# Depthwise convolution taps of a diffusion backbone: four per pass on TensorE, fewer on GpSimd and VectorE

## The reference, cut to what matters

```python
def conformer_conv(h, w_in, b_in, w_dw, b_dw, ln_g, ln_b, w_out, b_out):
    a, g = jnp.split(h @ w_in + b_in, 2, axis=-1)
    u = a * jax.nn.sigmoid(g)
    u = lax.conv_general_dilated(u, w_dw[:, None, :], window_strides=(1,),
        padding=[(CONV_K // 2, CONV_K // 2)],
        dimension_numbers=("NWC", "WIO", "NWC"),
        feature_group_count=D_CONV) + b_dw
    # a layer norm over the channels, silu, and a product with w_out follow
```

## Time and profile before

| | |
|---|---|
| median of three runs | 1851.17 us (1850.03 to 1855.13) |
| profiled execution: span from the first to the last instruction | 1854.0 us |
| TensorE matmul busy | 1803.4 us, 97% of the span |
| VectorE busy | 1198.1 us, 65% |
| ScalarE busy | 619.6 us, 33% |
| GpSimd busy | 171.7 us, 9% |
| chain that ended last: TensorE, VectorE, GpSimd | 84%, 6%, 4% of the span |

### The profile page before, as it was taken

The page is one execution under the profiler, slowest core; times in us unless marked ns, Lnnn a source line. Parts: engine busy times, 40 slices in busy tenths (PEclk is TensorE's granted clock), DMA queues, the critical chain, the costliest instruction groups (busy, mean ns, idle before and its releaser), DMA issues.

```text
span 1854.0 us, 22066 instructions
## 1 busy us (share of the span) xinstructions
PE 1803.4 (97%) x8604; PEld 1486.5 (80%) x8604; DVE 1198.1 (65%) x1541; ACT 619.6 (33%) x796; POOL 171.7 (9%) x148
## 2 busy tenths in 40 slices
PE   5899999998999999999999999999999999999999
PEld 2688888888898888888988888889764898888888
DVE  5876767667867676666676766547798555444454
ACT  2522222234342223222432222225776542222221
POOL 0000000002110000000200000002995200000000
PEclk8999999998999999999999999999999999999999
DMA  7753634431436354363154353411120321313201
GB/s 279 273 201 114 212 127 155 185 113 47 136 114 227 114 176 164 122 218 114 69 196 145 140 200 113 136 68 46 46 91 25 116 88 69 136 68 113 90 23 69
DMA packets 160395, 238.10 MB, mean 128 GB/s; under 512 B 3805, under 2 KB 110509, under 8 KB 160204
## 3 DMA queue, kind: packets, MB, share of 16 engines
q1 hardware_dynamic: 160016, 236.99, 36.5%
q10 hardware_dynamic: 316, 0.23, 0.0%
HBM read 235.11 MB, written 2.10 MB: 128 GB/s over the span
## 4 chain that ended last, share of the span: by engine, by line
PE 84%; DVE 6%; POOL 4%; ACT 3%; DMA 1%; issue 1%; SPq 0%; POOLq 0%; DVEq 0%; ACTq 0%
PE bank L1670 15%; PE bank L1672 15%; PE bank L1677 15%; PE bank L1545 10%; PE bank L1547 10%; PE bank L1546 10%; POOL tmp_c L628 3%; DVE mod_acc L1025 2%; PE bank L1927 1%; DVE w_lo L992 1%; PE bank L1617 1%; PE bank L1615 1%; PE bank L1619 1%; DMA raw_pair<-in_w_mod 1%; POOL sq_sum L593 1%
## 5 line engine op out<-in xcount | busy, mean ns | idle before, releaser
L1670 PE MATMUL bank<-a_hi,w_hi 128*128 128x512 f32 x1408 | 551.9, 392 | 6.2 <-ACT a_hi L686 4.7
L1672 PE MATMUL bank<-a_hi,w_lo 128*128 128x512 f32 x1408 | 548.9, 390 | 0.0
L1677 PE MATMUL bank<-a_lo,w_hi 128*128 128x512 f32 x1408 | 434.5, 390 | 1.3 <-DVE a_lo L1100 1.2
L1670 PEld LDWEIGHTS bank<-a_hi,w_hi 128*128 128x128 f32 x1408 | 265.0, 188 | 63.4 <-issue 6.3
L1218 DVE SCALAR_TENSOR_TENSOR h<-bank,half_gate,h 128x512 f32<-128x512 f32 x320 | 233.3, 745 | 121.7 <-PE bank L1547 121.1
L1677 PEld LDWEIGHTS bank<-a_lo,w_hi 128*128 128x128 f32 x1408 | 264.6, 188 | 57.3 <-DVE a_lo L1100 2.3
L1672 PEld LDWEIGHTS bank<-a_hi,w_lo 128*128 128x128 f32 x1408 | 264.9, 188 | 56.2 <-issue 1.4
L1545 PE MATMUL bank<-p_hi,w_hi 128*128 128x512 f32 (+1 forms) x768 | 289.5, 377 | 1.5 <-DVE h L1225 0.9
L1547 PE MATMUL bank<-p_lo,w_hi 128*128 128x512 f32 (+1 forms) x768 | 287.5, 374 | 0.0
L1546 PE MATMUL bank<-p_hi,w_lo 128*128 128x512 f32 (+1 forms) x768 | 287.4, 374 | 0.0
L992 DVE TENSOR_TENSOR w_lo<-raw_pair,w_hi 128x2048 fp32r<-128x2048 f32 x102 | 235.4, 2308 | 51.8 <-ACT w_hi L800 47.9
(11 more groups left out here) (197 smaller groups left out, 1849.2 us busy)
## 6 DMA issues: line engine op xcount, KB each, us to landing
raw_pair<-in_w_ff_in SPq DMA_DIRECT2D x88, 1024.0 KB, 7.0
raw_mod<-in_w_mod SPq DMA_DIRECT2D x66, 1024.0 KB, 8.4
raw_down<-in_w_ff_out SPq DMA_DIRECT2D x44, 1024.0 KB, 8.6
raw_pair<-in_conv_w_in SPq DMA_DIRECT2D x8, 1024.0 KB, 6.8
raw_pair<-in_w_mod SPq DMA_DIRECT2D x6, 1024.0 KB, 16.0
raw_pair<-in_fnet_w_out SPq DMA_DIRECT2D x4, 1024.0 KB, 6.1
raw_pair<-in_conv_w_out SPq DMA_DIRECT2D x4, 1024.0 KB, 6.7
raw_mod<-in_x SPq DMA_DIRECT2D x4, 512.0 KB, 5.6
```

The costliest lines, as they stand in the source:

```text
L1670: pe.matmul(ps[banks + s][:], tile_hi, a_hi[:, k], start=k == 0, stop=False, skip_group_check=True)
L1672: pe.matmul(ps[banks + s][:], tile_lo, a_hi[:, k], start=False, stop=False, skip_group_check=True)
L1677: ins = pe.matmul(ps[banks + s][:], w_hi[b][:, s * KD + k], a_lo[:, k], start=False, stop=k == KD - 1, skip_group_check=True)
```

## The change

The shares of the taps change. `QUADS` is 4: a "set" `s` stands for the four taps `s`, `s+8`, `s+16`, `s+24`. Blocks 0 to 5 have 3 sets (12 taps) on TensorE, 8 products on ScalarE and GpSimd, 11 taps on VectorE; block 6 has 5 sets (20), 8 and 3; block 7 has 6 sets (24), 4 and 3.

For a set, TensorE contracts over 128 rows that hold 32 channels four times, each copy of `u` shifted by 8 tokens more than the one before; the stationary operand is 128x32 and the result has 32 channels. Four such matmuls, for the four groups of 32 channels, go to the four column tiles of the array (`tile_position=(0, 32 * g)`) and write the four quarters of the same bank. The moving data, `u_rep`, is made by 16 DMAs per block on SyncE's queue (`replicate_u`), from `u_pad`, in two buffers that take the place of `p_hi` and `p_lo`; the tap weights are replicated once in the same way (`wdw_rep`). The stationary operands of all sets of a block are written by one GpSimd instruction (`tap_matrices`), which stands behind GpSimd's second add of the block before.

TensorE's order becomes: inputs of blocks 0, 1 and 2, taps of 0 and 1, input of 3, taps of 2, and so on. Block 0 starts its even sum in a bank of its own too. ScalarE loses the tap matrices, and the sigmoid stands behind all products in every block.

```diff
@@ shares of the taps
-    NE = 5
-    SIGMOID_EARLY = 5
     LAST_IN_AT = 7
-    SPLIT = [(NE, 11)] * (KD - 2) + [(13, 8), (17, 9)]
-    PE_TAPS = [list(range(e)) for e, _ in SPLIT]
+    QUADS = P // 32
+    TAP_STEP = 8
+    SPLIT = [(3, 8)] * (KD - 2) + [(5, 8), (6, 4)]
+    MOST_SETS = max(n for n, _ in SPLIT)
+    LEFT_TAPS = [[TAP_STEP * j + s for s in range(n, TAP_STEP) for j in range(QUADS)
+                  if TAP_STEP * j + s < TAPS] for n, _ in SPLIT]
+    POOL_TAPS = [left[:p] for left, (_, p) in zip(LEFT_TAPS, SPLIT)]
+    DVE_TAPS = [left[p:] for left, (_, p) in zip(LEFT_TAPS, SPLIT)]
+    TU = T + MOST_SETS - 1
...
+        u_rep = p_both[:].bitcast(F32).rearrange("p (b g x) -> p b g x", b=2, g=QUADS)
+        wdw_rep = mod_split[:].bitcast(F32).rearrange("p a (b x) -> p (a b) x", b=2)
...
+        APART_BANK = {0: Y_SUM_BANK, KD - 1: 0}
@@ SyncE
-            for j in (2, 3):
-                conv_converted(2 * j - 4)
-                conv_converted(2 * j - 3)
-                conv_pair(j, PAIR[CONV] + j)
+            def replicate_u(ch):
+                sp.wait_ge(s_u, ch + 1)
+                if ch >= 2:
+                    sp.wait_ge(s_pe_tap, ch - 1)
+                for j in range(QUADS):
+                    for g in range(QUADS):
+                        sp.dma_start(u_rep[32 * j:32 * (j + 1), ch % 2, g],
+                                     u_pad[32 * g:32 * (g + 1), ch % 3, TAP_STEP * j:TAP_STEP * j + TU]).then_inc(
+                                         s_u_rep[ch % 2], 16)
+            sp.wait_ge(s_vec, NV + 2)
+            sp.wait_ge(s_mod_sum, 2 * NMU - 2)
+            wdw_flat = wdw[:].rearrange("p k t -> p (k t)")
+            for j in range(QUADS):
+                for g in range(QUADS):
+                    sp.dma_start(wdw_rep[32 * j:32 * (j + 1), g, 0:KD * TAPS - TAP_STEP * j],
+                                 wdw_flat[32 * g:32 * (g + 1), TAP_STEP * j:]).then_inc(s_wdw_rep, 16)
+            conv_converted(0)
+            conv_converted(1)
+            conv_pair(2, PAIR[CONV] + 2)
+            replicate_u(0)
+            replicate_u(1)
+            conv_converted(2)
+            conv_converted(3)
+            conv_pair(3, PAIR[CONV] + 3)
             for q in range(2):
+                replicate_u(2 * q + 2)
+                replicate_u(2 * q + 3)
                 conv_converted(2 * q + 4)
                 conv_converted(2 * q + 5)
                 wo_pair(conv_w_out, q, PAIR[CONV] + 4 + q)
+            replicate_u(6)
+            replicate_u(7)
@@ GpSimd
+            def tap_matrices(ch):
+                if ch >= 2:
+                    pool.wait_ge(s_pe_tap, ch - 1)
+                n = SPLIT[ch][0]
+                shape = [P, n, QUADS, 32]
+                pool.tensor_tensor(
+                    tap_mats[:, ch % 2, 0:n].rearrange("p s (g c) -> p s g c", g=QUADS),
+                    stack[:].unsqueeze(1).unsqueeze(1).to_broadcast(shape),
+                    wdw_rep[:, :, ch * TAPS:ch * TAPS + n].rearrange("p g s -> p s g").unsqueeze(3).to_broadcast(shape),
+                    ALU.mult).then_inc(s_diag_tap, 1)
...
+            tap_matrices(0)
             adds = 0
...
                     adds += 1
+                    if j == 1 and ch + 1 < KD:
+                        tap_matrices(ch + 1)
@@ ScalarE
-            for j in range(NE):
-                tap_matrices(0, j)
...
-                    if j >= begin:
-                        for m in range((j - begin) * per, min((j - begin + 1) * per, matrices)):
-                            tap_matrices(ch + 1, m)
-                    if j == products - 1 - (SIGMOID_EARLY if ch == KD - 2 else 0) and ch + 1 < KD:
-                        sigmoid(ch + 1)
+                if ch + 1 < KD:
+                    sigmoid(ch + 1)
@@ VectorE
-                apart = c1 == KD - 1
+                apart = c1 in APART_BANK
                 bank = ps[4 + c1 % 2][:]
-                even, odd = ps[0][:] if apart else bank, ps[6][:]
+                even, odd = ps[APART_BANK[c1]][:] if apart else bank, ps[6][:]
@@ TensorE
-                n = len(PE_TAPS[ch])
-                for j, tap in enumerate(PE_TAPS[ch]):
-                    pe.wait_ge(s_diag_tap, before(ch, PE_TAPS) + j + 1)
-                    ins = pe.matmul(ps[4 + ch % 2][:], tap_matrix(ch, j), u_pad[:, ch % 3, tap:tap + T],
-                                    start=j == 0, stop=j == n - 1, skip_group_check=True)
+                pe.wait_ge(s_diag_tap, ch + 1)
+                pe.wait_ge(s_u_rep[ch % 2], 16 * QUADS * QUADS * (ch // 2 + 1))
+                n = SPLIT[ch][0]
+                for s in range(n):
+                    for g in range(QUADS):
+                        rows = slice(32 * g, 32 * (g + 1))
+                        ins = pe.matmul(ps[4 + ch % 2][rows, :], tap_mats[:, ch % 2, s, rows],
+                                        u_rep[:, ch % 2, g, s:s + T], start=s == 0, stop=s == n - 1,
+                                        tile_position=(0, 32 * g), skip_group_check=True)
                 ins.then_inc(s_pe_tap, 1)
...
-                if ch >= 1:
+                if ch == 2:
+                    conv_taps(0)
+                if ch >= 2:
                     conv_taps(ch - 1)
             conv_taps(KD - 1)
```

More of the change, by code:

```diff
@@ L69, in hybrid_backbone @@
     assert NI == 11 and UNIT_STEPS[2] == 8
-    NE = 5
-    SIGMOID_EARLY = 5
     LAST_IN_AT = 7
-    SPLIT = [(NE, 11)] * (KD - 2) + [(13, 8), (17, 9)]
-    PE_TAPS = [list(range(e)) for e, _ in SPLIT]
-    POOL_TAPS = [list(range(e, e + p)) for e, p in SPLIT]
-    DVE_TAPS = [list(range(e + p, TAPS)) for e, p in SPLIT]
-    assert sum(e - NE for e, _ in SPLIT) <= 20
+    QUADS = P // 32
[7 more added lines that the diff above has]
+    TU = T + MOST_SETS - 1
+    assert MOST_SETS < TAP_STEP and QUADS * TAP_STEP == TAPS + 1
     def before(ch, taps, less=0):
@@ L180, in hybrid_backbone @@
         a_lo = sb("a_lo", [P, KD, T], F32R)
-        p_hi = sb("p_hi", [P, 2, 2, T], F32R)
-        p_lo = sb("p_lo", [P, 2, 2, T], F32R)
+        p_both = sb("p_both", [P, 2 * QUADS * TU], F32R)
+        p_hi, p_lo = [p_both[:, n * 4 * T:(n + 1) * 4 * T].rearrange("p (a b n) -> p a b n", a=2, b=2)
+                      for n in range(2)]
         w_hi = [sb(f"w_hi{b}", [P, 16, P], F32R) for b in range(3)]
@@ L188, in hybrid_backbone @@
         mod_acc = sb("mod_acc", [P, MU])
[L189 to L190 removed]
+        mod_split = sb("mod_split", [P, 2, MU], F32R)
+        mod_acc_hi, mod_acc_lo = mod_split[:, 0], mod_split[:, 1]
         tmp_a = sb("tmp_a", [P, 2, T])
@@ L195, in hybrid_backbone @@
         u_pad = sb("u_pad", [P, 3, T + 2 * HALO])
-        tap_mats = sb("tap_mats", [P, 2, NE, P])
-        tap_last = sb("tap_last", [P, 4, P])
+        tap_mats = sb("tap_mats", [P, 2, MOST_SETS, P])
+        stack = sb("stack", [P, 32])
         ident = sb("ident", [P, P])
@@ L369, in hybrid_backbone @@
         s_term = sem("terms_ready")
+        s_stack = sem("stacked_identity_ready")
+        s_wdw_rep = sem("replicated_taps_loaded")
+        s_u_rep = [sem(f"replicated_u_loaded{n}") for n in range(2)]
         s_diag_tap = sem("tap_matrices_ready")
@@ L387, in down_weights, with merges @@
             return w_ff_out[f // 2, f % 2].rearrange("(j p) n -> p j n", p=P)
[L389 to L394, removed]
+        def merges(ch):
+            return sum(2 if c in APART_BANK else 1 for c in range(ch + 1))
         def layer_unit(unit):
@@ L582, in _ @@
                                pattern=[[-1, P]], channel_multiplier=1).then_inc(s_const, 1)
+            pool.wait_ge(s_const, 8)
+            pool.tensor_tensor(stack[:], ident[:, 0:32], ident[:, 32:64], ALU.add).then_inc(s_stack, 1)
+            for g in range(2, QUADS):
+                pool.wait_ge(s_stack, g - 1)
+                pool.tensor_tensor(stack[:], stack[:], ident[:, 32 * g:32 * (g + 1)], ALU.add).then_inc(s_stack, 1)
+            def tap_matrices(ch):
[8 more added lines that the diff above has]
+                    ALU.mult).then_inc(s_diag_tap, 1)
             def square_add(n, hf, o):
@@ L611, in _ @@
             ff_square_adds(4)
+            pool.wait_ge(s_stack, QUADS - 1)
+            pool.wait_ge(s_wdw_rep, 16 * QUADS * QUADS)
+            tap_matrices(0)
             adds = 0
@@ L636, in pair_lo @@
                                    ALU.subtract).then_inc(s_w[b], 1)
-            pool.wait_ge(s_merge, KD + 1)
+            pool.wait_ge(s_merge, merges(KD - 1))
             pair_lo(WO_UNITS[CONV][0], PAIR[CONV] + 4, 0)
@@ L912, in _ @@
             ff_norm(4, 1, 3, lambda: pair_hi(FIRST[CONV][1], PAIR[CONV], 1))
[L914 to L920, removed]
             def sigmoid(ch):
@@ L934, in _ @@
                 act.wait_ge(s_u, ch + 1)
[L935 to L938, removed]
                 for j, tap in enumerate(POOL_TAPS[ch]):
@@ L1502, in _ @@
                     dve.tensor_tensor(y_conv[:, c1], y_conv[:, c1], even, ALU.add).then_inc(s_merge, 1)
```

(17 more changed lines are left out.)

2 lines of the change are left out of this document (removed).

## The result

| | before | changed |
|---|---|---|
| median | 1850.6 us (1849.9 to 1855.1) | 1879.1 us (1877.3 to 1882.6) |
| ratio | | 1.015, 95% interval 1.0136 to 1.0163 |
| span of the profiled execution | 1854.0 | 1875.5 |
| TensorE matmul busy | 1803.4 | 1819.3 |
| VectorE, ScalarE, GpSimd busy | 1198.1, 619.6, 171.7 | 1176.1, 587.6, 146.0 |

The change is slower by 28 us where 14 faster was forecast. Three engines have less work, as they should; TensorE alone has more. In which part of the program? Two marks cut the execution in three: the end of the inputs of blocks 0 and 1, and the end of the last merge.

What follows compares the result with a forecast made beforehand. GpSimd bounds today at 16.4 us a block; TensorE would bound at 13.5. The last merge comes 22 us before today's 1421.3; less 8 of allowances, 14 are won, so the median becomes 1837, range 1829 to 1860.

Steps and rivals of the forecast that it cites:

- as today: Start of the convolution on TensorE: the first two input blocks end at 1297.2 us, unchanged.
- keeps its order and moves as a whole: Program behind the last merge: cost unchanged, so the convolution's gain passes whole to the median.
- allowances: Four deductions from the 22 us won: clock 2.5, array draining 2, late copies 2, GpSimd's matrices 1.5; together 8.
- The set of four matmuls: Taps on TensorE: four column tiles run together, 0.87 us a set; bounds 0.87 and 3.48.
- Pairs: Rival, taps on TensorE: tiles overlap only two records at a time, set 1.74 us, time 1848; chance 0.30.
- None together: Rival, taps on TensorE: column tiles don't overlap, set 3.48 us, 43 slower, 1894; chance 0.12.
- GpSimd's matrices: One GpSimd instruction per block writing stationary operands: 1.1 us for 384 elements; bounds 0.8 and 4.5.
- The issue of a copy: SyncE's queue: 0.42 us each, 6.7 for 16, so a copy is ready 8.8 after its `u`.
- The clock: Last taps on TensorE: after a wait of 6 the clock may fall to half, adding 0 to 5 us; taken 2.5.
- The middle cycle: TensorE's block in mid-convolution: input 10.9 plus three sets of 0.87, 13.5 us, against 16.4 on GpSimd today.
- copies late behind loads: SyncE's queue: copies of blocks 2, 4 and 6 behind a 2 MB load, 0 to 4 us; taken 2.

Runs made afterwards that it cites:

- aligned: Also written after_aligned: changed kernel with room for 520 instead of 517 elements per copy, so tiles behind start at multiples of 64 bytes again; 1839.5 us.
- before_rest32: Kernel before with 32 unused bytes per partition behind the weight tiles, moving only what follows them; 1850.9 us, ratio 0.9996.
- before_all64: Kernel before with 64 unused bytes ahead of `h`, shifting moving and stationary operands alike; 1852.2 us, ratio 1.0007.
- before_w32: Kernel before with 32 unused bytes per partition ahead of the weight tiles; 1890.3 us, ratio 1.0205.
- before_w64: Kernel before with 64 unused bytes per partition ahead of the weight tiles; 1888.1 us, ratio 1.0199.
- before_moving64: Kernel before with 64 unused bytes ahead of `h` and 64 more ahead of the weight tiles, so only moving operands start off 128; 1886.9 us, ratio 1.0186.
- aligned_two_queues: Changed kernel with realigned weight tiles, 8 of the 16 copies of block 7 issued on ScalarE's queue ahead of its products; 1833.2 us, ratio 0.99.

## Why the prediction was wrong

**The step that failed** is the frame of the sum, in two sentences: the first two input blocks end "as today", and what comes after the last merge "keeps its order and moves as a whole". Both take the rest of the program to cost what it did, and neither was argued. No instruction there is changed, but its operands' addresses are. They cost 39.6 us (the changed kernel against the aligned one); no rival had that, and the range ended 19 below the result. The 160 bytes could have been read from the diff: 517 elements, eight times, ahead of the weight tiles.

**The sum for the convolution** can be held against the runs step by step, counted from the end of the first two inputs:

| us | forecast | changed | aligned |
|---|---|---|---|
| taps of block 0 end | 13.6 | 13.9 | 13.6 |
| taps of block 1 begin | 16.0 | 19.0 | 19.0 |
| taps of block 1 end | 18.6 | 23.1 | 24.4 |
| taps of block 2 end | 33.9 | 37.2 | 38.2 |
| input of block 7 ends, taps of block 6 begin | 85.5 | 90.9 | 91.0 |
| taps of block 7 begin | 95.8 | 104.1 | 105.1 |
| last merge ends | 101.7, 109.7 with allowances | 111.7 | 113.6 |

- The set of four matmuls was taken at 0.87 and is 0.88. *Pairs* and *None together* fall. The records' own starts show how: four begin within 0.02 us (1354.868 to 1354.888), the next four 0.43 later. The rival read the program-order rule that the prediction cites from the Trainium skill (TensorE: Matmul & The Clock Gate, "The mechanism") so that a tile's second record stands ahead of the next tile's first; this trace differs from that reading. Which record is of which tile it doesn't say, so whether the rule itself is broken stays open.
- GpSimd's matrices, taken at 1.1 and feared at 3 to 4.5, are 0.86. VectorE and GpSimd don't bound.
- The issue of a copy was taken at 0.42 and is 0.63. It was read off small loads from HBM and large ones, of which none goes from SBUF to SBUF. A copy of block 7 is ready 11.4 after the end of its `u` instead of 8.8 (12.4 in the aligned kernel, whose last 16 issues stand 0.69 apart). That is 2.6 at block 7; at block 1, where two blocks' copies stand in a row, the taps begin 3 later than forecast.
- The clock, 2.5 as an allowance for one place, struck in two: 2.6 (5.35 - 2.79) at block 1 and 2.3 (7.65 - 5.37) at block 7 in the aligned kernel. The forecast has a wait of only 2.4 at block 1 and no fall of the clock in it; it was 5.1, and 5.4 in the aligned kernel. There the taps behind both waits take longer than in the changed kernel (5.35 and 7.65 against 4.10 and 6.83), which is part of why its convolution is 1.9 longer; what makes them longer there isn't shown.
- The middle cycle, 13.5, is 13.8 to 14.0 with aligned tiles and 14.11 without.

So with tiles where they had been, the forecast of 1837 would have been off by 2.5 us, with a gain of 11.4 where 14 was said. The mechanism inside the convolution was right and two of its terms too small. That the sum comes so near is in part luck: of the allowances, 2 for copies late behind loads and 1.5 for the matrices were not needed (TensorE waits for no copy of blocks 2, 4 or 6), and they cover part of what issue and clock cost more. The time was decided elsewhere.

## What to carry to other kernels

A change of a tile's size moves every tile behind it; ahead of any estimate, compare the start addresses of matmul operands before and after, and keep the distance between moving and stationary tiles as it was; of the changes to it tried here, only one of 256 bytes cost nothing. When time changes where nothing was edited, count instructions in a saturated stretch: the busy share stays at 100%, the count doesn't. Many small copies on one queue cost their issue, 0.63 us each here, and a wait for them can be paid twice, the second time in the clock of what follows.

## What the runs showed of the hardware

- fp32r matmuls of 128x512 start 227 ns apart with the distance between moving and stationary operands as in the kernel before (before, before_rest32, before_all64) or 256 bytes larger (after_aligned), and 233 ns apart where it is 32, 64 or 160 larger (before_w32, before_w64 and before_moving64, after). Those of 256 columns start 120 ns apart in the former and 116 to 120 in the latter.
- Of four float32 matmuls of 128x32 in four column tiles, four records start within 0.02 us, and the four matmuls take 0.88 us together (after) against 0.87 for one of 128x128 (before).
- SyncE issues SBUF-to-SBUF copies of 64.6 KB 0.63 us apart (after). Beside each other SyncE needs 0.64 a copy and ScalarE 0.68 (aligned_two_queues).
- A GpSimd product of two broadcast operands takes 0.86 us for 384 elements per partition and 1.53 for 768 (after).
